# Expert results written straight to token order, and read back by plain loads

## The reference

```python
g_top = argmax(xf @ w_rg + b_rg)                      # 1 of 4 groups for each token
top_vals, top_idx = top_k(e_logits[g_top], 2)         # 2 of its 8 experts
weights = p_g * softmax(top_vals)
expert = g_top * 8 + top_idx                          # 32 experts, 1024 (token, choice) pairs
def run_chunk(xc, e):
    return (silu(xc @ w_gate[e]) * (xc @ w_up[e])) @ w_down[e]
out = segment_sum(ys * row_w, row_tok)                # each token: its two rows, weighted
```

## Time and profile before

| | us |
|---|---|
| median of 3 runs | 1748.86 (1748.4 to 1750.69) |
| the profiled execution's own time | 1747.27 |
| its span in the profile | 1745.3 |
| TensorE busy | 1568.0 |
| VectorE busy | 552.8 |
| ScalarE busy | 350.1 |

### The profile page before, as it was taken

One profiled execution on the slowest core, in us unless ns is written; L12 is line 12 of the kernel. 1 busy time (PEld: TensorE's weight loads), 2 busy tenths in 40 slices (PEclk: granted clock), 3 DMA queues, 4 the chain that ended last, 5 costly groups with the idle time before them and its releaser, 6 DMA issues. The chain is left out here.

```text
span 1745.3 us, 17682 instructions
## 1 busy us (share of the span) xinstructions
PE 1568.0 (90%) x6788; PEld 726.7 (42%) x6788; DVE 552.8 (32%) x1412; ACT 350.1 (20%) x723; POOL 46.1 (3%) x43
## 2 busy tenths in 40 slices
PE   7999978999998999939999899996999998999970
PEld 3444444444433343325654455553444443333330
DVE  3111344212221212155263687345121212121124
ACT  2000121111110111121342577422111110111111
POOL 0000010000000000020000000010000000000002
PEclk9999988999999999969999899997999999999995
DMA  6273228999999999973310300307999999999974
GB/s 193 72 277 132 64 97 342 420 421 421 420 421 420 421 421 421 393 214 97 97 49 1 145 1 1 146 16 281 419 421 420 421 421 421 420 422 421 420 287 158
DMA packets 116244, 482.33 MB, mean 276 GB/s; under 512 B 23600, under 2 KB 50224, under 8 KB 66224
## 3 DMA queue, kind: packets, MB, share of 16 engines
q1 hardware_dynamic: 103440, 455.55, 64.8%
q10 hardware_dynamic: 10400, 17.05, 2.6%
q0 software_dynamic: 2304, 8.39, 1.3%
HBM read 457.62 MB, written 23.33 MB: 276 GB/s over the span
## 5 line engine op out<-in xcount | busy, mean ns | idle before, releaser
L797 PE MATMUL ps<-raw,e_xT 128*64 128x512 f32 x2080 | 466.2, 594 | 47.2 <-DMA raw<-in_expert_w_up 47.2
L797 PEld LDWEIGHTS ps<-raw,e_xT 128*64 128x64 f32 x2080 | 156.2, 137 | 347.9 <-issue 347.4
L877 DVE TENSOR_TENSOR e_hid<-e_sg,ps 64x512 f32<-64x512 f32 x65 | 44.1, 679 | 637.8 <-ACT e_sg L844 637.8
L821 PE MATMUL ps<-raw,e_hT 128*64 128x512 f32 x1040 | 237.5, 598 | 0.0
L407 PE MATMUL ps<-c_hT,raw 128*128 128x512 f32 x384 | 165.0, 592 | 0.2 <-ACT c_hT L350 0.2
L844 ACT ACTIVATE e_sg<-ps 64x512 f32<-64x512 f32 x65 | 38.7, 596 | 467.6 <-PE ps L797 467.6
L771 PE MATMUL ps<-m_xhi,e_pick 128*128 128x512 f32 x276 | 118.9, 431 | 9.6 <-DVE e_pick L859 9.6
L821 PEld LDWEIGHTS ps<-raw,e_hT 128*64 128x64 f32 x1040 | 68.9, 136 | 122.3 <-issue 111.4
L1409 PE MATMUL ps<-a_spare,raw 128*128 128x512 f32 x256 | 113.6, 600 | 1.5 <-ACT a_spare L1116 1.5
L771 PE MATMUL ps<-m_xlo,e_pick 128*128 128x512 f32 x276 | 111.5, 404 | 0.0
L407 PEld LDWEIGHTS ps<-c_hT,raw 128*128 128x128 f32 x384 | 72.9, 190 | 91.7 <-issue 91.4
(11 more groups left out here) (218 smaller groups left out, 1270.5 us busy)
## 6 DMA issues: line engine op xcount, KB each, us to landing
raw<-in_expert_w_gate SPq DMA_DIRECT2D x130, 1024.0 KB, 27.2
raw<-in_expert_w_up SPq DMA_DIRECT2D x130, 1024.0 KB, 27.3
raw<-in_expert_w_down SPq DMA_DIRECT2D x130, 1024.0 KB, 27.5
slots_y<-e_ysb ACTq DMA_DIRECT2D x130, 128.0 KB, 6.8
raw<-in_conv_w_in SPq DMA_DIRECT2D x12, 1024.0 KB, 10.3
raw<-in_w_kv SPq DMA_DIRECT2D x6, 1024.0 KB, 7.4
raw<-in_conv_w_out SPq DMA_DIRECT2D x1, 4096.0 KB, 19.0
slots_y<-c_zero SPq DMA_DIRECT2D x16, 256.0 KB, 13.0
```

Of the source, the lines that this page charges most:

```text
L797: mm = pe.matmul(ps_gu[C - C * i:2 * C - C * i, :], xT[:, q % 2, k, u * C:(u + 1) * C], ring(m, L, p)[:, kk * F:(kk + 1) * F], start=(k == ...
L821: mm = pe.matmul(ps_y[c % 2][n * C:(n + 1) * C, :], hT[:, 2 * h + kk, :], ring(m, L, p)[:, kk * D + n * 512:kk * D + (n + 1) * 512], start ...
L877: dve.tensor_tensor(hid[:], sg[:], ps_gu[0:C, :], ALU.mult).then_inc(s_hid, 1)
```

## The change

- Each layer has its own DRAM buffer `pairs_y` of 1024 rows in token order: row 2 x token + choice. ACT copies a chunk's result in two halves into 64 partitions of 1024 columns, and POOL writes the 64 rows with one indirect DMA to the rows in `to_row`. Empty slots get a row number out of bounds, and the DMA drops them.
- The row numbers are found on the way: `code` holds 2 x token + 1 and a clamped slot for each token; with every second half of a gather TensorE multiplies the four `pick` tiles with it (two columns each), and `dve_dest` turns the products into row numbers, two chunks at a time.
- When the last scatter has landed, SP loads the rows back inside the experts' block, four loads of 1 MB, one for each tile with both choices. The gathers are gone, so are `m.idx`, `slots_y` and the zero stores.
- Each norm's Newton step takes two operations in place of four; the mean is kept times -0.5 and ACT's root scales by -2.
- The questions for overflow chunks are nested: `1 < n` is asked inside `0 < n`, and so on, so the first that fails ends them all. POOL now goes through the chunks too.

```diff
@@ -45,7 +45,7 @@
 KF = F // P
 C = 64
 N_OVF = 2 * S // C
-ROWS = (E + N_OVF) * C
+FAR = 4096.0
 NPIECE = 6
 PIECE = 2048
 NR = 16
...
+        m.part = sb("part", [P, 1])
+        m.to_row = sb("to_row", [C, E + N_OVF + PAIR], U32)
         m.wts = sb("wts", [P, NT, 2])
         m.novf = sb("novf", [1, 1], I32)
         m.ovf_e = sb("ovf_e", [1, N_OVF + 1], I32)
         m.banks = ctx.enter_context(nc.psum_tensor("ps", [P, 8, 512], F32))
         m.ps = [m.banks[:, i, :] for i in range(8)]
-        m.slots_y = nc.dram_tensor("slots_y", (ROWS, D), F32, kind="Internal").ap()
+        m.pairs_y = [nc.dram_tensor(f"pairs_y{L}", (2 * S, D), F32, kind="Internal").ap() for L in range(2)]
         m.ready = sem("constants_ready")
+        m.come = [[sem(f"k{L}_in{t}") for t in range(NT)] for L in range(2)]
         m.load = {}
 
...
@@ -186,14 +190,25 @@
             pool.memset(m.ones[:], 1.0).then_inc(filled, 1)
             pool.iota(m.iota[:], [[1, GS]], base=0, channel_multiplier=0,
                       allow_small_or_imprecise_dtypes=True).then_inc(filled, 1)
-            pool.wait_ge(filled, 3)
+            pool.iota(m.part[:], [[1, 1]], base=0, channel_multiplier=1,
+                      allow_small_or_imprecise_dtypes=True).then_inc(filled, 1)
+            pool.wait_ge(filled, 4)
             pool.affine_select(out=m.ident[:], in_=m.ident[:], compare_op=ALU.not_equal, fill=1.0, base=0,
                                pattern=[[-1, P]], channel_multiplier=1).then_inc(filled, 1)
             pool.affine_select(out=m.before[:], in_=m.ones[:], compare_op=ALU.is_gt, fill=0.0, base=0,
                                pattern=[[1, P]], channel_multiplier=-1).then_inc(filled, 1)
-            pool.wait_ge(filled, 5)
+            pool.wait_ge(filled, 6)
             pool.tensor_copy(m.identb[:], m.ident[:]).then_inc(m.ready, 1)
             pool.wait_ge(m.ready, 1)
+
+        @block.vector
+        def _(dve):
+            dve.wait_ge(filled, 4)
+            for i in range(2 * NT):
+                c = dve.tensor_scalar(m.code[:, i // NT, i % NT, 0:1], m.part[:], 2.0, float(2 * P * (i % NT) + 1),
+                                      ALU.mult, ALU.add)
+            c.then_inc(m.coded, 1)
+            dve.wait_ge(m.coded, 1)
 
 
 class Norm:
...
-        act.activation(m.rstd[:, self.n, t:t + 1], m.ss[:, 4 + t:5 + t], ACT.Sqrt).then_inc(self.rt, 1)
+        act.activation(m.rstd[:, self.n, t:t + 1], m.ss[:, 4 + t:5 + t], ACT.Sqrt, scale=-2.0).then_inc(self.rt, 1)
 
     def vector_mean(self, dve, t):
 
         m = self.m
         dve.wait_ge(self.sq, t + 1)
-        dve.tensor_scalar(m.ss[:, 4 + t:5 + t], m.ss[:, t:t + 1], 1.0 / D, EPS, ALU.mult, ALU.add).then_inc(self.ms, 1)
+        dve.tensor_scalar(m.ss[:, 4 + t:5 + t], m.ss[:, t:t + 1], -0.5 / D, -0.5 * EPS, ALU.mult, ALU.add).then_inc(self.ms, 1)
 
     def vector_root(self, dve, t):
 
@@ -231,10 +246,8 @@
         dve.wait_ge(self.rt, t + 1)
         own.step(dve.reciprocal(rs, rs))
 
-        own.step(dve.tensor_tensor(tmp, rs, rs, ALU.mult))
-        own.step(dve.tensor_tensor(tmp, tmp, ms, ALU.mult))
-        own.step(dve.tensor_scalar(tmp, tmp, -0.5, 1.5, ALU.mult, ALU.add))
-        own.step(dve.tensor_tensor(rs, rs, tmp, ALU.mult))
+        own.step(dve.scalar_tensor_tensor(out=tmp, in0=rs, scalar=rs, in1=ms, op0=ALU.mult, op1=ALU.mult))
+        own.step(dve.scalar_tensor_tensor(out=rs, in0=tmp, scalar=1.5, in1=rs, op0=ALU.add, op1=ALU.mult))
 
     def vector_normed(self, dve, xn, t):
...
-        self.come = [m.sem(f"k{L}_in{i}") for i in range(2 * NT)]
-
-    def gathers(self, pool):
-        m = self.m
-        for t in range(NT):
-            for k in range(2):
-                pool.indirect_dma_start(out=m.rows_y[:, t, k, :], out_offset=None, in_=m.slots_y[:, :],
-                                        in_offset=bass.IndirectOffsetOnAxis(ap=m.idx[:, t, k:k + 1], axis=0)
-                                        ).then_inc(self.come[2 * t + k], 16)
+        self.come = m.come[L]
 
     def vector_add(self, dve, t, k):
         m = self.m
-        dve.wait_ge(self.come[2 * t + k], 16)
+        dve.wait_ge(self.come[t], 16)
         if k:
             dve.wait_ge(self.own, t + 1)
...
-            blank = [m.slots_y[i * P:(i + 1) * P, :] for i in range(E * C // P, ROWS // P)]
-            for rows in blank:
-                for h in range(2):
-                    sp.dma_start(rows[:, h * S:(h + 1) * S], zero[:]).then_inc(s_blank, 16)
             sp.wait_ge(s_proj, 3 * NK)
             r.sync_weights(sp)
             prefetch(sp, m, 0, (6, 7))
             r.sync_ring(sp)
-            sp.wait_ge(s_blank, 32 * len(blank))
 
         @block.scalar
...
-            dve.tensor_copy(m.idx[:], m.slot[:]).then_inc(self.s_slots, 1)
+            dve.tensor_reduce(m.slot[:].rearrange("p t k -> p k t"), self.oh, AX.X, ALU.add).then_inc(self.s_slots, 1)
             dve.wait_ge(self.s_slots, 1)
...
+        sg_hid = sb("sg_hid", [P, F])
+        hid, sg = sg_hid[0:C, :], sg_hid[C:P, :]
         hT = sb("hT", [P, KF, C])
-        ysb = sb("ysb", [P, 2, D // 2])
+        ysb = sb("ysb", [C, 2, D])
+        dest = m.ss[:, 0:2]
...
+                wait(pe, s_row, 2 * q)
+                for t in range(NT):
+                    mm = pe.matmul(ps_d, pick[:, q % 2, t, :], m.code[:, q % 2, t, :], start=(t == 0), stop=(t == NT - 1))
+                mm.then_inc(s_dest, 1)
 
         def pe_turn(pe, n):
 
...
             wait(act, s_hid, c)
-            act.activation(sg[:], ps_gu[C:2 * C, :], ACT.Silu).then_inc(s_sg, 1)
+            act.activation(sg, ps_gu[C:2 * C, :], ACT.Silu).then_inc(s_sg, 1)
             act_rows(act, c + PAIR)
             wait(act, s_used, c * NPIECE + 6)
-            wait(act, s_st[c % 2], c // 2 * 32)
-            act.activation(ysb[:, c % 2, :], ps_y[c % 2][:], ACT.Copy).then_inc(s_yev, 1)
-            act.wait_ge(s_yev, c + 1)
+            wait(act, s_st[c % 2], c // 2 * 16)
             for n in range(2):
-                act.dma_start(m.slots_y[c * C:(c + 1) * C, n * 512:(n + 1) * 512], ysb[n * C:(n + 1) * C, c % 2, :]
-                              ).then_inc(s_st[c % 2], 16)
+                y = act.activation(ysb[:, c % 2, n * 512:(n + 1) * 512], ps_y[c % 2][n * C:(n + 1) * C, :], ACT.Copy)
+            y.then_inc(s_yev, 1)
+
+        def pool_step(pool, c):
+
+            wait(pool, s_row, c + 1)
+            wait(pool, s_yev, c + 1)
+            pool.indirect_dma_start(out=m.pairs_y[L][:, :], in_=ysb[:, c % 2, :], in_offset=None,
+                                    out_offset=bass.IndirectOffsetOnAxis(ap=m.to_row[:, c:c + 1], axis=0),
+                                    bounds_check=2 * S - 1, oob_is_err=False).then_inc(s_st[c % 2], 16)
 
         def dve_pick(dve, own, g):
 
             wait(dve, s_rg, 2 * (g - 1))
+            wait(dve, s_dest, g - 1)
+            dve.tensor_scalar(m.code[:, g % 2, :, 1], m.slot[:, :, 0], -1.0, float(GS), ALU.max, ALU.min).then_inc(s_code, 1)
             for t in range(NT):
                 own.step(dve.tensor_scalar(pick[:, g % 2, t, :], m.iota[:], m.slot[:, t, 0:1], None, ALU.is_equal))
                 dve.scalar_tensor_tensor(out=pick[:, g % 2, t, :], in0=m.iota[:], scalar=m.slot[:, t, 1:2],
                                          in1=pick[:, g % 2, t, :].bitcast(F32), op0=ALU.is_equal, op1=ALU.add
                                          ).then_inc(s_pick, 1)
             dve.wait_ge(s_pick, NT * (g + 1))
+            dve.wait_ge(s_code, g + 1)
             own.step(dve.tensor_scalar(m.slot[:], m.slot[:], float(GS), None, ALU.subtract))
+
+        def dve_dest(dve, own, g):
+
+            dve.wait_ge(s_dest, g + 1)
+            token, choice = ps_d[:, 0:1], ps_d[:, 1:2]
+            own.step(dve.tensor_scalar(dest[:, 0:1], choice, m.part[:], None, ALU.not_equal))
+            own.step(dve.tensor_tensor(dest[:, 0:1], dest[:, 0:1], token, ALU.add))
+            own.step(dve.tensor_scalar(dest[:, 1:2], token, 0.0, FAR, ALU.is_equal, ALU.mult))
+            for u in range(PAIR):
+                half = slice(u * C, (u + 1) * C)
+                dve.scalar_tensor_tensor(out=m.to_row[:, PAIR * g + u:PAIR * g + u + 1], in0=dest[half, 0:1], scalar=-1.0,
+                                         in1=dest[half, 1:2], op0=ALU.add, op1=ALU.add).then_inc(s_row, 1)
 
         def dve_turned(dve, n):
 
@@ -874,13 +896,15 @@
 
             wait(dve, s_sg, c + 1)
             wait(dve, s_ht, c)
-            dve.tensor_tensor(hid[:], sg[:], ps_gu[0:C, :], ALU.mult).then_inc(s_hid, 1)
+            dve.tensor_tensor(hid, sg, ps_gu[0:C, :], ALU.mult).then_inc(s_hid, 1)
             wait(dve, s_ht, c + 1)
             wait(dve, s_used, c * NPIECE)
             dve.tensor_copy(hT[:].rearrange("p k c -> p (k c)"), ps_h[:, 0:KF * C]).then_inc(s_hev, 1)
             dve_turned(dve, c + PAIR)
             if c % PAIR == 0:
                 dve_pick(dve, own, c // PAIR + 2)
+            else:
```

(27 more changed lines are left out.)

35 lines of the change are left out of this document (15 added, 20 removed).

## The result

The kernel after takes 1698.54 us (median of four runs, 1694.96 to 1700.7), the kernel before 1748.63 on the same chip: a ratio of 0.9713, 95% interval 0.9702 to 0.9725. The prediction said 1728 with a range of 1702 to 1735. The direction was right, the size was not: 50 us were gained where 20.6 were forecast. The profiled execution of after took 1697.77 us, 1.77 of it outside its span.

The account below looks back on a forecast made before the run. Full DMA engines bound the expert stages, latency the layer ends. Terms -1.0 - 0.8 + 1.0 + 0 - 5.5 - 14.3 = -20.6 take 1747.27 to 1726.7, plus 1.6 for the median 1728.3; range 1702 to 1735.

Parts of the forecast that it names:

- Expert chunks, DMA: Result stores in the DMA-bound expert stages: dropping empty slots' rows gains 0, with 22.7 us as the other bound.
- blocks of neighbouring rows: Expert-stage stores: rows dealt to engines in blocks, so the first engine still carries four full rows per chunk; gain 0.
- stores halve: Rival 1, expert-stage stores: rows dealt evenly or dropped ones made up, another -22.7 us, 1705.6; chance 0.32.
- Expert chunks, TensorE: Destination products cost 0.5 us a pair, hidden by DMA except before each layer's first chunk: +1.0 us in all.
- Start and routers: Kernel start: cheaper setup and shorter norms, -1.0 us; routers: last tile's norm 0.39 a layer, -0.8 in all.
- End of layer 0: Last copy to next stage: scatter, early row loads, no wait for the second sum, shorter norms; -5.5 us (-2 to -7).
- End of layer 1: Last copy to final scalings: nested questions remove the hole, but scaling waits for the final gain's load; -14.3 us.
- 2 (the walk isn't shortened): End of layer 1: nesting leaves TensorE's walk over skipped chunks, only 7.8 us saved there, 1734.8; chance 0.07.
- 3 (scatters dearer): Expert stages: scatters cost more than stores, 0.70 to 1.0 us a chunk, 1729 to 1745; chance 0.06.
- 4 (slower): Expert stages: scatters on saturated engines cost over 1.02 us a chunk, kernel slower than before, 1761 at 1.2; chance 0.05.

Follow-up runs that it names:

- the first 32: Kernel after with fixed row numbers: only partitions 0 to 31 of each chunk are written, results miss their tokens; 1696.32 us, 0.971.
- every second partition: Kernel after with fixed row numbers: only even partitions of each chunk are written, results miss their tokens; 1696.39 us, 0.9711.
- 32 bytes less: Kernel after with the small table `part` folded into another, so ten ring places start 224 past a multiple of 256; 1712.79 us, 0.9803.
- the kernel with the gain on ACT's queue: Kernel after with the load of the final gain issued by ACT instead of SP, at the head of the last stage; 1698.09 us, 0.9708.
- all rows written: Kernel after with empty slots' rows sent to spare rows instead of dropped, so every chunk writes 64 rows; 1716.34 us, 0.9823.
- before with 32 bytes more: Kernel before with an unused 32-byte table behind the small ones, so ten ring places start at a multiple of 256; 1737.99 us, 0.9947.

## Why the prediction was wrong

**Expert chunks, DMA: this is the step that failed.** The prediction took 0, with 22.7 as the other bound; the stages got 25.6 us shorter, by two gains that add up. First, dropped rows: it chose "blocks of neighbouring rows", by which the fullest engine would store four rows of every chunk as before. The runs with the first 32 and with every second partition have the same time, and writing all rows gives 19.2 us back, 15.1 of them in the stages. What the prediction draws from the Trainium skill, "DMA: Bandwidth & Descriptors", section "Why a DMA increments its semaphore by 16 and not by 1", is equal shares of rows. The 0 needs more: that a share is a block of neighbouring partitions, and that the lowest partitions always fall to the same engines. For these scatters that doesn't hold, by the two runs. The packet records show what a dropped row is: between 570 and 706 us the scatters of nine chunks left 287 packets of 4 KB (159.1 ns each) and 433 of 4 bytes (9 ns each); 144 of these are the sixteen with which each DMA ends, and 289 are the nine times 32 empty slots, with one more at the window's edge. A dropped row stays a packet and costs an eighteenth of a row. How the rows are dealt to the engines is not seen. The rival "stores halve" had the mechanism right, at 0.32 of chance, with 22.7 us for it and the time of 1705.6.

Second, the start address of the ring, which no sentence of the prediction looks at. It is worth 10.4 us of the stages from before's side and 11.7 from after's; over the whole kernel the medians say 9.3 and 15.7. Of that difference between the two sides the stages hold only 1.3 us, and the rest wasn't explained; part of it can be chance, since the stretch between the two expert stages takes 469.3 us in after and 471.2 in the kernel with the gain on ACT's queue, which are alike there. The kernel after without this gain (32 bytes less) takes 1712.79 us, which lies in the prediction's range: its chance for halved stores would have covered the dropping, and nothing in it covered the address.

Measured one by one, dropping (19.2), the address (9.3), the nested questions (15.4) and the roots (4.4) add up to 48.3 of the 50 us.

**Expert chunks, TensorE** (+1.0): a pair's products cost 0.2 us, not 0.5, by the early distance. The direction was right, the term too large. That DMA hides them holds: the stages of all rows written, with these products, are as long as those of before with 32 bytes more, without them.

**Start and routers** (-0.9 to the first Silu of layer 0 with the first pair's products): -2.1. The first product of the convolution came 1.15 us earlier, as predicted (-1.0). The kernel with the roots alone has its first Silu 1.66 earlier; the rest is small and wasn't followed, and kernels with nothing but a padding differ by up to 1.1 at this point. One reading was off: the zero stores did not lie only where DMA is under half busy (its share is 0.93 from 100 to 150 us), but TensorE is busy for the whole 50 us, so they were worth about 0 all the same.

**End of layer 0** (-5.5): -6.1. First sum 8.7 us after the last copy's end, where the text had 9.5: from the copy's end SP could load after 4.0 us, where 4.4 were taken, and the load took 4.8, as predicted.

**End of layer 1** (-14.3): -15.5. Every part of it was there: no hole, first sum 8.8 us after the last copy's end (9.4 in the text), and the wait for the gain of 2.67 (about 3). But here the early loads have little part. From the overflow chunk's Silu to the end of the span it is 56.6 us before, 40.5 with the nested questions alone (gathers kept, the gain loaded ahead of them), 41.2 in after, and 38.5 in after with the gain as the third load. So the nested questions are worth the whole term; the shorter roots (1.4 here, by the kernel with them alone) and the early loads only make up for the wait for the gain.

**The other rivals.** 2 (the walk isn't shortened), 3 (scatters dearer) and 4 (slower) did not happen. (The upper end of rival 3 would be 1748 by its own 1.0 us a chunk, not 1745.) A 4 KB packet of a scatter took 159.1 ns with the ring at a multiple of 256. With the ring at 224 past one it took 160.7, a plain one from ACT 159.7: POOL's queue is dearer by 0.6% a row, which doesn't count.

## What to carry to other kernels

Where DMA bounds a stage, add up the times of its packets: here an out-of-bounds row of a scatter cost 9 ns in place of 159.1, whichever partition held it. Before a change that adds or removes small tables is judged, look at the start of the large buffers behind them: one 32-byte table moved 0.5 to 0.9% of the time here, and without a test it would have been booked to whatever else the change did. And where several loads are waited for in order, put an additional one behind the last load that its user's engine needs before it: the final gain belonged behind the rows of the second tile.

## What the hardware showed that was not expected

- Weight packets of 8 KB take 309 ns where the tensor of most of the places starts at a multiple of 256 bytes in the partition, and 312.6 to 314.1 ns in the mean where it starts 64, 128 or 224 past one; 4 KB packets of the convolution's output weights take 159.0 ns at such a multiple and 164.5 to 164.8 at any of the other three.
- A dropped row of a scatter is a packet of 4 bytes and 9 ns, a written one 159.1 ns, at even partitions or at the lowest 32 alike.
- The profile's figure for the DRAM's written bytes counts dropped rows as written: 19.14 MB with and without dropping, where the packets of the queue have 8.40 and 17.04 MB.
- Two plain stores of 128 KB a chunk issued by POOL instead of ACT make the kernel 7 us longer, and none of that lies in the expert stages (931.4 against 931.6 us); 5 us of it lie at the end of layer 0, where the barrier opens later.
